# Shifting the experts' weight parts by 192 bytes, and TensorE's overfull loop written as nested conditions

## The reference

```python
N_EXPERTS = 8; TOP_K = 2; D_FF_EXPERT = 3584; MOE_BLOCK = 128
logits = (hf @ w_router).astype(jnp.float32)
top_vals, top_idx = lax.top_k(logits, TOP_K)
gates = jax.nn.softmax(top_vals, axis=-1)
...
def expert_block(args):
    xb, e = args
    return (jax.nn.silu(xb @ w_gate[e]) * (xb @ w_up[e])) @ w_down[e]
...
out = jnp.zeros_like(hf).at[tok].add(y)       # y = the token's row times its gate
```

## Time and profile before

| | |
|---|---|
| median of 3 runs | 2135.43 us (2135.2, 2135.43, 2141.47) |
| the profiled execution | 2142.29 us |
| its span, first to last instruction | 2140.5 us |
| mean granted clock of TensorE | 0.994 |
| PE busy | 2106.6 us, 98% |
| PEld busy | 1876.2 us, 88% |
| DVE busy | 1415.6 us, 66% |
| ACT busy | 1298.0 us, 61% |
| POOL busy | 651.9 us, 30% |

### The profile page before, as it was taken

The page is one execution under the profiler, slowest core; times in us unless marked ns, Lnnn a source line. Parts: engine busy times, 40 slices in busy tenths (PEclk is TensorE's granted clock), DMA queues, the critical chain, the costliest instruction groups (busy, mean ns, idle before and its releaser), DMA issues.

```text
span 2140.5 us, 33470 instructions
## 1 busy us (share of the span) xinstructions
PE 2106.6 (98%) x13271; PEld 1876.2 (88%) x13275; DVE 1415.6 (66%) x1431; ACT 1298.0 (61%) x1427; POOL 651.9 (30%) x316
## 2 busy tenths in 40 slices
PE   9999999999999999999999999999999999999997
PEld 8979999988999898999998888888888888888886
DVE  1455223336422684323777999999999999999996
ACT  4556445455645544444545777777777777777775
POOL 5726885726788102988201000000000000000000
PEclk9999999999999999999999999999999999999999
DMA  7434554625455334555446999999999999999994
GB/s 244 135 115 151 173 190 146 185 68 160 159 193 178 107 113 138 197 196 191 134 150 215 383 376 335 375 356 377 352 344 378 361 365 344 364 357 376 357 369 181
DMA packets 307635, 529.09 MB, mean 247 GB/s; under 512 B 11842, under 2 KB 152802, under 8 KB 307520
## 3 DMA queue, kind: packets, MB, share of 16 engines
q1 hardware_dynamic: 306496, 525.92, 70.1%
q0 software_dynamic: 736, 1.00, 0.2%
q10 hardware_dynamic: 288, 0.52, 0.1%
HBM read 525.84 MB, written 1.05 MB: 246 GB/s over the span
## 4 chain that ended last, share of the span: by engine, by line
PE 86%; POOL 5%; DVE 4%; ACT 2%; issue 2%; DMA 0%; POOLq 0%; SPq 0%; DVEq 0%; ACTq 0%
PE bank L718 84%; POOL weights_low L3001 5%; PE bank L1460 1%; DVE qb L2269 1%; ACT sc L1600 1%; DVE sc L2269 1%; PE bank L892 0%; DVE sc L2277 0%; DMA ring<-in_w_ple_dram 0%; ACT weights_high L1603 0%; DVE nmax L2304 0%; DVE h L2277 0%; DVE y L2277 0%; ACT expert_weights_high L1603 0%; ACT sq L1600 0%
## 5 line engine op out<-in xcount | busy, mean ns | idle before, releaser
L2269 DVE TENSOR_TENSOR expert_weights_low<-ring_experts,expert_weights_high 128x2048 fp32r<-128x2048 f32 x336 | 764.8, 2289 | 72.5 <-ACT expert_weights_high L1603 72.3
L1603 ACT ACTIVATE expert_weights_high<-ring_experts 128x2048 fp32r<-128x2048 f32 x336 | 646.6, 1925 | 166.2 <-PE bank L718 162.1
L3001 POOL TENSOR_TENSOR weights_low<-ring,weights_high 128x1024 fp32r<-128x1024 f32 x252 | 617.3, 2472 | 354.9 <-ACT weights_high L1603 354.8
L1603 ACT ACTIVATE weights_high<-ring 128x1024 fp32r<-128x1024 f32 x294 | 303.7, 1056 | 333.1 <-PE bank L718 293.0
L718 PE MATMUL bank<-x_high,weights_high 128*128 128x256 f32 x1024 | 246.9, 282 | 1.1 <-POOL weights_low L3001 1.1
L718 PE MATMUL bank<-x_high,weights_low 128*128 128x256 f32 x1024 | 243.8, 279 | 0.0
L718 PEld LDWEIGHTS bank<-x_high,weights_high 128*128 128x128 f32 x1024 | 193.3, 189 | 2.6 <-DVE zs L2277 1.5
L718 PEld LDWEIGHTS bank<-x_high,weights_low 128*128 128x128 f32 x1024 | 193.3, 189 | 0.6 <-issue 0.5
L718 PE MATMUL bank<-expert_weights_high,gathered_high 128*128 128x512 f32 x456 | 180.7, 396 | 0.3 <-DVE gathered_low L2277 0.3
L718 PE MATMUL bank<-expert_weights_high,gathered_low 128*128 128x512 f32 x456 | 177.8, 390 | 0.0
L718 PE MATMUL bank<-expert_weights_high,gathered_high_b 128*128 128x512 f32 x448 | 177.6, 396 | 0.0
(11 more groups left out here) (331 smaller groups left out, 3739.5 us busy)
## 6 DMA issues: line engine op xcount, KB each, us to landing
ring_experts<-in_moe_w_gate_dram SPq DMA_DIRECT2D x112, 1024.0 KB, 6.5
ring_experts<-in_moe_w_up_dram SPq DMA_DIRECT2D x112, 1024.0 KB, 6.3
ring_experts<-in_moe_w_down_dram SPq DMA_DIRECT2D x112, 1024.0 KB, 5.9
ring<-in_w_in_dram SPq DMA_DIRECT2D x62, 1024.0 KB, 5.2
ring<-in_w_merge_dram SPq DMA_DIRECT2D x24, 1024.0 KB, 5.1
ring<-in_w_out_dram SPq DMA_DIRECT2D x14, 1024.0 KB, 5.4
ring<-in_ffn_w_gate_dram SPq DMA_DIRECT2D x11, 1024.0 KB, 5.1
ring<-in_ffn_w_up_dram SPq DMA_DIRECT2D x11, 1024.0 KB, 5.2
```

Source lines behind the costliest of these rows:

```text
L1603: return nc.scalar.activation(dst, src, ACT.Copy, scale=scale)
L2269: return nc.vector.tensor_tensor(dst, x, z, op)
L3001: nc.gpsimd.tensor_tensor(half_of(wlo[:, q_slot, :], t, width), half_of(ring[:, slot, :], t, width), half_of(whi[:, q_slot, :], t, width). ...
```

## The change

An unused tile of 48 float32 (192 bytes) is declared in front of `expert_weights_high`. The two weight-part tiles then start at 180096 and 204672, which is 128 modulo 256, while `gathered_*` and `hidden_turned_*` stay at 192; the last byte used is 229248 of 229376. On TensorE the loop over overfull turns becomes a condition that holds the turn and the next condition, three deep, with Python numbers in place of the loop's register. So where `over_n` is 0, one comparison passes all three bodies, which stand in the program one after another. The other engines' loops stay.

```diff
         lsum = over[:, 3, :]
+        sb("between_operands", [P, 48], m2)
         ewh = sb_r("expert_weights_high", [P, SPLITS_E, SLOT], m2)
         ewl = sb_r("expert_weights_low", [P, SPLITS_E, SLOT], m2)
...
             add_up(EXPERTS - 1)
-            with pe.Fori(0, OVER) as k:
+
+            def overfull(k):
                 with pe.If(n_over > k):
                     finish(k + (EXPERTS - 1))
                     pe.wait_ge(comb.h, comb.at(k + EXPERTS, 0))
                     first_step(k + EXPERTS, k + PAIRS, (0, 0))
                     expert(k + EXPERTS, k + PAIRS, (0, 0))
                     add_up(k + EXPERTS)
+                    if k + 1 < OVER:
+                        overfull(k + 1)
+
+            overfull(0)
```

## The result

The changed kernel is slower by one per cent, a small change but clear of the noise: 2158.81 us median (2156.88 to 2162.34, 4 runs) against 2138.45 (2135.2 to 2142.97, 4 runs) of the kernel before beside it, a ratio of 1.0101 with an interval of 1.0077 to 1.0125. The forecast was 2131.7 us in a range of 2127 to 2146: wrong in sign and outside the range. It went as rival A said, and more dearly.

What follows compares the result with a forecast made beforehand. TensorE's back-to-back instructions were taken to bound the experts' stage, with TensorE's queue and SP's waits at the very end. From 2135.43 us, 0 - 1.3 + 0 - 2.4 = -3.7 gave 2131.7, range 2127 to 2146.

Steps and rivals of the forecast that it cites:

- rival A: Experts' stage: the shift brings a lasting slow spacing to the long matmuls, 4.5 ns each, 18 us, 2151 us; chance 0.20.
- Part 1: Experts' undisturbed 512-column matmuls: going from distance 0 to -64 keeps their spacing of 227 ns, change 0.
- Part 2: Experts' matmuls just behind breaks such as transposes: their slow steps get cheaper, -1.3 us, in bounds of 0 to -2.7.
- Part 3: VectorE and ScalarE with the moved weight parts: any slowing up to 8% is covered, taken at 0.
- Part 4: Loop over overfull experts at the end: one comparison of 3.4 us removes SP's wait for TensorE, -2.4 us.
- The sum: Whole kernel: 0 - 1.3 + 0 - 2.4 = -3.7 us, giving 2131.7 us.
- The base: Whole kernel before: median 2135.43 us of three runs, from which the forecast starts, with 2 us allowed for few runs.

Runs made afterwards that it cites:

- The probes: Kernels of TensorE alone, the computation left out, timing matmuls by distance and width; at 512 columns 226.7 ns at distance 0, 233.3 at -64.
- loop alone: Changed kernel without the unused tile, only the nested conditions: 2136.64 us (10 runs), 0.9994 of the kernel before.

## Why the prediction was wrong

**Part 1** is the step that failed. It had the right rows: the two levels at -64, the slower one alone at +64, distance 0 at 512 columns with a slow spacing that dies out. It then divided 227 by two, found 113.3, and took the two as the same level "column for column", so that a move from distance 0 to -64 changed nothing. That needs two assumptions which no row carried: that the loss is proportional to columns, and that the effect of a distance is the same at each width. The probes refute both: at distance 0 the loss was 13.3 ns at 256 columns as at 512, and -64, the best at 256, cost 6.7 ns at 512. In the kernel the term was to be 0 and measured +6.0 ns a step, 22.9 us. Its own rows held a warning: for 256 columns -64 had two levels, and a level that can last is a risk which distance 0 at 512 columns, where the slow steps always died out, didn't have.

**Rival A** was the mechanism: "if the new distance brings the lasting kind to the long matmuls". Its price was 4.5 ns x 4032 = 18 us; measured are 6.0 ns and 22.9 us. The 4.4 came from 256 columns, the 5 from the steps behind a break, and neither is the level at -64 and 512 columns. Its argument against itself, that a 512-column matmul leaves its load room, was wrong: in the probe the long matmuls run slower at -64 than at 0 with no other engine at work. A chance of 0.20 looks too low, where the only two facts on the new state (a lasting slow level at -64, a dying one at 0) both pointed to it.

**Part 2** took half of 2.7 us off the steps behind breaks. They became no cheaper. They stand at 233 where they stood at 231.7, and no longer differ from the others.

**Part 3** holds: 2290 ns for 2289.

**Part 4** holds in its mechanism and is mis-sized downwards. One record at the condition is left, 3.8 us for the 3.4 that were taken; SP's wait for TensorE fell from 2.5 to 0.2 us, the 2.4 forecast within a tenth. But the end shortened by 3.6 us in the kernel after and 3.8 in loop alone. The term that was mis-sized is the output transfer, bounded at 0 to 1 us and taken at 0: from SP's first issue to the last landing it took 6.4 us before, 5.1 after and 5.0 in loop alone. In the kernel before, the branch of 7567 ns, from 2131.5 us on the earlier trace rows, lies over that whole stretch. With nested conditions the one branch ends before SP's first issue, or within 0.03 us of it, and the stretch is 4.6 to 5.4 us in all eight such traces. That fits the guess that the jump disturbs the transfers, but no run separates the two. One reading was also wrong: the first branch does not stand behind TensorE's last matmul. It starts at 2127.4 us, and the last matmul at 2128.8.

**The sum.** 22.9 - 3.6 = 19.3 us, against 20.4 in the medians. Had part 1 been at 6.0 ns, the prediction's own working would have given 2135.4 + 24 - 2.4 = 2157.

**The base.** The three runs of before that were shown lie between 2135.2 and 2141.5, and 2 us were added for that; 22 runs spread over 19 us. The cause is in the earlier trace rows: whether the 256-column matmuls fall into 113.3 or 117.7 differs from run to run, and this alone would be worth 6500 x 4.4 = 29 us between the extremes; the traces seen lie between a share of 32% and one of 69% at the slower level. It isn't what put the result outside the range.

**The Trainium skill's rule** that PE never waits, "SBUF — State Buffer", section "Who interferes with whom", would have given no change from the shift. The runs speak against it, by 23 us.

**A better version.** None was found that beats the kernel before clearly. The nested conditions without the shift stand at 0.9994 (0.9975 to 1.0014), and with all tiles of the stage moved together at 0.9984 (0.9969 to 0.9998): 2 to 3 us, somewhat less than the end shows, and hardly more than a measurement resolves. The layout of before was already at the best distances of those tried, 0 at 512 columns and -64 at 256.

**Open.** Why the good distance depends on the width; what decides between 113.3 and 117.8 at -64 and 256 columns (not the number of transposes in front: 3 of them gave 113.3 once and 117.8 twice in the first two probes, 5 gave each once; behind 6, 7 and 8 it was 113.3 in both probes that had them); what in TensorE makes the loss; and whether widths and distances that were not tried do better.

## What to carry to other kernels

Where TensorE is the bound and streams fp32r against fp32r loads back to back, measure the spacing for the very pair of width and address distance in use before a tile is moved: 1 ns a step was 4 us here, and -64, the best distance tried at 256 columns, cost the 512-column matmuls 2.6% of their spacing. Don't carry a level from one width to another because the ratio looks round; a run of 32 matmuls of TensorE alone gave the kernel's spacing within 0.6 ns. And a stream that has two levels needs more than two or three runs before its better one is counted on.

## What the runs showed of the hardware

A matmul's spacing depends on where its moving tile lies relative to its standing tile, modulo 256 bytes, with no other engine at work. For fp32r at a granted clock of 1.00 (2.4 GHz), the last steps of a run:

| moving minus standing | 512 columns, ns | 256 columns, ns |
|---|---|---|
| 0 | 226.7 | 119.3 to 120.0 |
| +16 | 231.7 | 113.3 twice, then 116.4 to 118.8 |
| +32 | 233.3 | 116.7 to 117.8 |
| +64 | 228.8 to 228.9 | 117.8 |
| 128 | 232.6 to 232.9 | 118.4 to 119.1 |
| -64 | 233.3 | 113.3 or 117.8 |
| -48 | 234.5 to 234.8 | 118.7 to 119.4 |

The steps settle into a pattern that repeats (226, 227, 227 at 0; 226, 229, 232 at +64; 231, 236 or 233, 233, 234 at -64) and held to the end of these runs of 16 to 32. Against columns / 2.4 GHz, 213.3 and 106.7 ns, the loss is 13 to 23 (with -16, 236.7 in one run) and 7 to 13 ns; the bfloat16 matmuls of the earlier trace rows lose 4.

And a branch on TensorE's queue that passes a large body can take microseconds. Of the three of the kernel before, two are in the earlier trace rows; all three (ns min/median/max):

```profile
L1588 PEldq COMPARE_BRANCH  x3: 221/3392/7567, 2127.4 to 2139.7; - x3
```

So two took 3.4 and 7.6 us, and the third, over the same body, 0.22. The one over three bodies took 3.8 us in the kernel after and 3.7 to 4.2 in the eight kernels that have it, so its price didn't grow threefold with what it passes. The Trainium skill has a reason under "Runtime: NRT & Kernel Launch", section "Instruction fetch mechanics": a taken branch out of the window that is loaded has to fetch its target first. The long records fit that; no row shows the fetch itself, and why the third was short stays open.
